# The first rows' second layer begun on three of its four low parts, and three pieces of side work moved in a hybrid decoder step

## The reference, cut to what matters

```
h   = rmsnorm(x);  z = h @ w_in                       # one projection for both head groups
o_g = gated linear attention, 4 heads, 64-token blocks
o_d = (softmax(q1 k1^T) - lambda softmax(q2 k2^T)) v  # 4 heads, causal; the 8 running
                                                      # sequences read 16 cached pages each
x   = x + concat(o_g, o_d) @ w_out
u   = square(relu(rmsnorm(x) @ w_up))                 # 1024 -> 4096
x   = x + u @ w_down                                  # 4096 -> 1024
```

## Time and profile before

| | |
|---|---|
| time, median of 3 runs | 1398.96 us (1396.02 to 1400.2) |
| profiled execution, its own time | 1402.99 us |
| its span, first to last instruction | 1401.3 us |
| PE busy | 1354.2 us (97%) |
| DVE busy | 904.4 us (65%) |
| ACT busy | 576.9 us (41%) |
| POOL busy | 399.6 us (29%) |
| mean granted TensorE clock | 0.994 of full speed |

### The profile page before, as it was taken

How to read it: one execution, slowest core, us unless ns; L and a number is a source line. 1 busy time by engine, 2 the same in 40 slices (tenths; PEclk the granted TensorE clock), 3 DMA queues, 4 the chain that set the end, 5 groups by cost and what they waited for, 6 DMA issues and landing times.

```text
span 1401.3 us, 23890 instructions
## 1 busy us (share of the span) xinstructions
PE 1354.2 (97%) x8589; PEld 1124.1 (80%) x8589; DVE 904.4 (65%) x1624; ACT 576.9 (41%) x1069; POOL 399.6 (29%) x395
## 2 busy tenths in 40 slices
PE   8999999999999989999999999999999999999998
PEld 6867777776777777777767766667999999999998
DVE  5469667745657777647667565525376665878785
ACT  6444333314544654524234241313444454334532
POOL 3546615435533444243000000000252212222020
PEclk9999999999999999999999999999999999999999
DMA  8447745444344665577386675874454564132301
GB/s 287 141 133 235 223 126 169 127 144 131 101 140 157 202 226 149 155 254 257 117 270 219 196 247 175 291 237 155 166 189 160 202 226 164 46 109 106 106 32 61
DMA packets 125543, 239.29 MB, mean 171 GB/s; under 512 B 13601, under 2 KB 46658, under 8 KB 125426
## 3 DMA queue, kind: packets, MB, share of 16 engines
q1 hardware_dynamic: 116226, 213.64, 46.6%
q10 hardware_dynamic: 9200, 24.13, 5.1%
HBM read 197.64 MB, written 40.09 MB: 170 GB/s over the span
## 4 chain that ended last, share of the span: by engine, by line
PE 60%; DVE 7%; issue 3%; ACT 2%; DMA 2%; POOL 1%; SPq 1%; ACTq 0%; DVEq 0%; POOLq 0%
PE ps L87 17%; PE ps L89 16%; PE ps L88 16%; PE ps L3316 2%; PE ps L1513 2%; PE ps L1550 1%; PE ps L1332 1%; DMA kr<-in_cache_k 1%; DVE uw_l L2036 1%; ACT uw_h L2030 1%; DVE sd L3070 1%; PE ps L1534 1%; DVE xt L2854 1%; DMA vr<-in_cache_v 1%; PE ps L1746 1%
## 5 line engine op out<-in xcount | busy, mean ns | idle before, releaser
L3081 POOL TENSOR_TENSOR kr<-kr,qb 128x512 f32<-128x512 f32 x128 | 171.8, 1354 | 171.8 <-DMA kr<-in_cache_k 171.5
L87 PE MATMUL ps<-x2hB,uw_h 128*128 128x264 f32 (+1 forms) x512 | 145.1, 283 | 0.7 <-DVE x2lB L2869 0.7
L88 PE MATMUL ps<-x2lB,uw_h 128*128 128x264 f32 (+1 forms) x512 | 144.7, 283 | 0.0
L89 PE MATMUL ps<-x2hB,uw_l 128*128 128x264 f32 (+1 forms) x512 | 144.5, 282 | 0.0
L87 PE MATMUL ps<-part_h,fh 128*128 128x264 f32 (+1 forms) x448 | 128.1, 286 | 4.5 <-DVE xt L2854 4.5
L89 PE MATMUL ps<-part_h,fl 128*128 128x264 f32 (+1 forms) x448 | 127.0, 284 | 0.0
L88 PE MATMUL ps<-part_l,fh 128*128 128x264 f32 (+1 forms) x448 | 126.9, 283 | 0.0
L87 PE MATMUL ps<-uh,dh 128*128 128x512 f32 x256 | 105.1, 411 | 8.2 <-DVE dl L2129 5.2
L3070 DVE TENSOR_REDUCE sd<-kr 128x8 f32<-128x512 f32 x128 | 85.0, 675 | 38.7 <-POOL kr L3081 38.6
L2854 DVE TENSOR_TENSOR xt<-xt,ps 128x264 f32<-128x264 f32 (+1 forms) x224 | 87.4, 422 | 34.2 <-PE ps L89 33.9
L87 PE MATMUL ps<-x2hA,uw_h 128*128 128x512 f32 x256 | 105.2, 411 | 0.0
(11 more groups left out here) (383 smaller groups left out, 3436.3 us busy)
## 6 DMA issues: line engine op xcount, KB each, us to landing
kr<-in_cache_k SPq DMA_DIRECT2D x128, 256.0 KB, 3.3
raw_up<-in_w_up_units SPq DMA_DIRECT2D x64, 512.0 KB, 4.7
vr<-in_cache_v SPq DMA_DIRECT2D x128, 256.0 KB, 3.6
raw_dn<-in_w_down SPq DMA_DIRECT2D x32, 512.0 KB, 6.3
raw_dn<-in_w_down ACTq DMA_DIRECT2D x32, 512.0 KB, 5.0
raw<-in_w_in_units SPq DMA_DIRECT2D x23, 512.0 KB, 5.7
raw_up<-in_w_out_units SPq DMA_DIRECT2D x16, 512.0 KB, 4.4
kept_up_low<-uw_l SPq DMA_DIRECT2D x14, 512.0 KB, 6.5
```

The source lines that it names most:

```text
L87: pe.matmul(out, lh, rh, start=first and n == 0, stop=False, skip_group_check=onto)
L88: pe.matmul(out, lh, rl, start=False, stop=False, skip_group_check=onto)
L89: ins = pe.matmul(out, ll, rh, start=False, stop=last and n == len(ks) - 1, skip_group_check=onto)
L3081: pool.tensor_tensor(k[:, :], k[:, :], qb[v // PAGES][:, :], ALU.mult).then_inc(k_multiplied, 1)
```

## The change

It does five things. `down` waits for three `dl` at its top and for the fourth, together with the fourth `ul`, after the six partial sums. ScalarE's side work of tick 19 stands ahead of the square of tile 1 of group 0 instead of behind its high part. VectorE's side work of tick 38 (tile 3 of group 1) stands behind `dl`, `xr` and `ul` instead of ahead of them. VectorE's side work of the ticks of group 1's `down` stands behind each addition instead of ahead of it. Step 13 of `keysB` moves from tick 16 to tick 17, where step 14 already stands.

```diff
         def down(g, tick):
-            pe.wait_ge(dn_low, FT * g + FT)
+            pe.wait_ge(dn_low, FT * g + 3)
             pe.wait_ge(u_low, up_no(g, 2) + 1)
...
             for o in range(2):
                 take(pe, "down", g, o)
                 sum_over(o, range(3), True, False)
+            pe.wait_ge(dn_low, FT * g + FT)
+            pe.wait_ge(u_low, up_no(g, 3) + 1)
             for o in range(2):
-                pe.wait_ge(u_low, up_no(g, 3) + 1)
                 sum_over(o, range(3, 4), False, True).then_inc(down_ready, 1)
...                                                    # scalar
+                if g == 0 and x == 1:
+                    beside(tick + 2 * x + 1)
                 i = up_no(g, x)
                 v = vt[:, i % 2, ALL]
                 act.wait_ge(v_made, i + 1)
                 act.activation(v, v, ACT.Square).then_inc(u_high, 1)
...
-                beside(tick + 2 * x + 1)
+                if g or x != 1:
+                    beside(tick + 2 * x + 1)
...                                                    # vector
-                beside(tick + 2 * x)
+                pages_last = (g, x) == (1, FT - 1)
+                if not pages_last:
+                    beside(tick + 2 * x)
                 down_low(g, x)
...
+                if pages_last:
+                    beside(tick + 2 * x)
                 beside(tick + 2 * x + 1)
...
             for o in range(KT):
-                beside(tick + 2 * FT + o)
+                if g != 1:
+                    beside(tick + 2 * FT + o)
                 dve.wait_ge(down_ready, down_no(g, o) + 1)
                 dve.tensor_tensor(xt[:, o, ALL], xt[:, o, ALL], ps[:, bank("down", g, o), :], ALU.add).then_inc(added, 1)
+                if g == 1:
+                    beside(tick + 2 * FT + o)
...                                                    # program: the table of ticks
-        put("keysB", [t0 + 2 + 41 * i // 37 for i in range(37)])
+        put("keysB", [t + (t == t0 + 2 * KT) for t in (t0 + 2 + 41 * i // 37 for i in range(37))])
```

## The result

The changed kernel takes 1403.04 us (median of 13 runs, 1400.47 to 1405.85), the kernel before 1399.09 us in the same runs. The ratio is 1.0028, with a 95% interval of 1.0020 to 1.0035. So it is about 4 us slower: a small loss, but the interval doesn't hold 1. The forecast was 1402.0, 3 us slower.

The account below looks back on a forecast made before the run. TensorE was taken as the bound, with a VectorE chain deciding from 506 to 513.5 us. Group 0 +6.4, group 1 -3.0 and the `down` split -0.4 gave +3.0 us on 1398.96: 1402.0 us, range 1396.5 to 1406.5.

Parts of the forecast that it names:

- The round trip of the key page: Group 0, VectorE at tick 18: waiting for page 92 takes 6.0 us from page 90's sum and delays `dl`.
- the normalisation: Group 0, POOL: the root starts earlier with the key product behind it, gaining 0.6 us (0.45 to 1.32).
- `stat`: Group 0, VectorE: this 1.05 us instruction no longer runs beside a POOL product, saving 0.7 us (0 to 0.8).
- the mix and the turn of unit 7: Group 0, VectorE then TensorE: both come 4.7 us later (bounds 3.4 to 8.5).
- ScalarE's edit: Group 0: `attn_t` is copied earlier, but TensorE then waits as much longer for the mix; cost and gain 0.
- The clock: Group 0, TensorE: the granted clock falls after an 8 us idle stretch, costing 1.7 us (0 to 3).
- the one precedent: Earlier trace: after a 2.88 us TensorE wait before 10.27, the clock was 0.72 from 10 to 16, losing 1.7 us.
- Group 1: TensorE's waits for `dl` and additions shrink, key page 112 then being late: gain 3.0 us (0.4 to 3.4).
- The split of `down`: Groups 2, 3 and 5: starting on three low parts gives 0.4 us in all (0 to 0.73).
- the two additions: Groups 3 and 5: first additions end a VectorE and ScalarE chain from `dl`, so removed waits return; gain 0.
- the 0.4 us counted for group 2: TensorE starts `down` 0.73 us earlier, but the addition of output 0 lets it keep only 0.4 us.
- The sum: Whole kernel: +6.4 - 3.0 - 0.4 = +3.0 us, giving 1402.0 us against the median; chance 50%.

Follow-up runs that it names:

- experiment 1: Kernel before with only key step 13 moved from tick 16 to tick 17: 1404.53 us, ratio 1.0039.
- experiment 2: Changed kernel with key step 13 put back at tick 16: 1399.23 us, ratio 0.9998 against the kernel before.
- experiment 5: Changed kernel with key step 15 also moved, from tick 18 to 19, behind the mix of unit 7: 1403.91 us, ratio 1.0037 against the kernel before.
- experiment 8: Kernel before with only ScalarE's side work of tick 19 moved ahead of the square: 1400.32 us, ratio 1.0008.
- Experiment 6: Changed kernel with 32 unused matmuls filling TensorE's long wait before the turn of unit 7: 1402.73 us, ratio 1.0027 against the kernel before.
- experiment 4: Kernel before with only group 1's VectorE side work moved behind `ul` and behind the additions: 1396.52 us, ratio 0.9982.
- experiment 3: Kernel before with only `down` begun on three of the four low parts: 1399.45 us, ratio 1.0002.
- experiment 7: Changed kernel with `down` begun on all four low parts again: 1404.19 us, ratio 1.0041 against the kernel before.
- experiment 9: Kernel before with only POOL's root of the normalisation moved ahead of its tick 16 side work: 1398.48 us, ratio 0.9991.
- experiment 10: Kernel before with group 1's VectorE side-work edits and POOL's root ahead of tick 16's side work: 1395.56 us, ratio 0.9969.
- experiment 11: Kernel before with group 1's edits, early root, `down` begun on three low parts, and output 0's addition earlier in every group: 1395.81 us, ratio 0.9971.
- experiment 12: Kernel before with group 1's edits, early root, split `down`, earlier output 0 addition, and ScalarE's tick 19 ahead of the square: 1395.91 us, ratio 0.9979.

## Why the prediction was right, point by point

**The round trip of the key page** was the right mechanism, shown by experiments 1, 2 and 5. No run gives the ring a third buffer, which would test it most directly. Its size came out right for a partly wrong reason, by luck. I had taken 6.0 us from the end of the sum of page 90 to the sum of page 92; it took 4.8 us (501.5 to 506.25), as the transfer took 2.57 us and not 3.4. The formula that the prediction quotes from the Trainium skill ("DMA: Bandwidth & Descriptors", Anatomy of one DMA) is given there for transfers that GpSimd issues, while SP issues these. Its 2.6 us fits the transfer of key page 92, and not that of key page 112, which took 5.0 us. What I had left out made up for the shorter trip. `dl` took 2.00 us instead of 1.2 and `ul` 1.81 instead of 0.7, each issued while POOL had just begun a product (506.51 and 510.80). In the prediction's own sum the terms were 6.0 for the trip, -0.6 for the normalisation and -0.7 for `stat`. They measured 4.8, -1.4 and -0.8, with 0.8 more for `dl` and 1.1 for `ul`: the mix and the turn of unit 7 came 4.5 us later, and I had said 4.7.

**The normalisation** gained the whole 1.3 us, not 0.6. I had put the value near the low end because the root took 2.00 us beside VectorE's splitting. In the changed kernel the root began 0.12 us ahead of the split of `uw_l`, took 1.02 us, and the split took 1.23 us (1.21 at 509.38, with POOL idle). By the rule of the Trainium skill ("SBUF — State Buffer", Who interferes with whom) the split should have been held until the root was over. It wasn't, so for this pair the trace disagrees. For `dl` and `ul` it agrees: `dl`, issued at 506.86 into a product that ends at 507.77, lasted until 508.86, 1.1 us after it.

**ScalarE's edit** gave nothing (experiment 8), for the reason stated.

**The clock** fell as the one precedent had let expect, for longer: 2.7 us in the trace instead of 1.7. Experiment 6 shows that the idle stretch is the cause of this fall: filled with work, it had none. In the same trace the clock fell a second time, in group 3 behind the wait of 2.19 us, which the prediction doesn't have:

```profile
718.00:720.00 2.00, 2.00 (x6) 1.57 (x5) 2.00 (x6) 0.88 (x2) 0.00 (x0) 0.52 1.03 405
720.00:722.00 2.00, 2.00 (x10) 1.29 (x9) 1.33 (x4) 1.44 (x2) 0.00 (x0) 0.63 1.05 381
```

**Group 1** was mis-sized in the changed kernel: of 3.4 us of waits 2.0 are left, a gain of 1.4 us instead of 3.0, as the round trip of key page 112 took 7.8 us. Alone the edits gave 2.7 us (experiment 4). What varied was the round trip, which I had seen range from 5.5 to 8.9 us; the forecast took 6.3 for it, and 8.9 only as a bound.

**The split of `down`** gave 0 in groups 3 and 5, as worked out from the two additions and shown by experiment 3. Of the 0.4 us counted for group 2 the traces show 0.05, and in all it gave nothing measurable.

**The sum.** Predicted +3.0 us, measured +4.0. The single edits measured against the kernel before give +5.3 + 0.2 - 2.7 + 1.4 = +4.2 us, each of them uncertain by 1.3 to 2 us. That forecast and time lie so near is in part luck: group 0 cost 7.2 us in the trace (forecast 6.4), group 1 gave back 1.4 (3.0) and the split nothing (0.4), which alone makes +5.8.

The two profiled executions differ by +6.5 us in block A, more than the medians do, and much of the excess is the clock, which doesn't fall alike in every execution. Experiments 3 and 4 don't touch group 0. TensorE has the same wait of 1.9 us for `attn_t` there, yet the clock fell behind it, and `down` of group 0 begins 0.9 us later than in the trace of the kernel before, which kept 1.00. In experiment 3:

```profile
508.00:510.00 2.00, 0.47 (x2) 0.47 (x3) 1.74 (x4) 1.74 (x6) 1.16 (x1) 0.91 1.00 261
510.00:512.00 2.00, 2.00 (x12) 2.00 (x11) 1.96 (x3) 1.06 (x1) 0.51 (x1) 0.50 0.96 354
512.00:514.00 2.00, 2.00 (x12) 1.87 (x12) 1.90 (x3) 0.53 (x2) 0.00 (x0) 0.74 1.04 412
```

The second fall in the changed kernel adds to it: from group 3's `down` to group 4's its trace takes 66.7 us, and experiment 3's, with the same split and no fall there, 66.0. Without these two the difference would be about 4.9 us, an estimate. The rest stays open.

## What to carry to other kernels

When a step of a pipelined side job is moved next to its neighbour, count the round trip of its buffer ring: with two buffers, everything between step `s` and step `s`+2 must last as long as a transfer and its processing, or an in-order engine stops there with all its other work. A wait that ends on an engine with its own chain (here `dl`, `ul`, the addition) wasn't removed by starting its user earlier. It came back under the next name with the same length, so look for what the chain itself depends on. Before a difference of 1 us between two traces is put down to an edit, compare the granted clock over the same stretch: here it fell in one execution and not in another with the same waits. Here the useful part of a coupled edit could be had by moving one instruction on the one engine where the conflict was.

## What the hardware showed that I had not expected

A root of 128x4 on POOL took 1.02 us beside VectorE's 128x1024 subtraction that began 0.12 us after it, and neither slowed the other. Seven more traces (experiments 5 to 7 and 9 to 12) show the same pair at 1.01 to 1.03 and 1.23 us. In the kernel before, the same root took 2.00 us when it began 0.55 us behind that subtraction, which itself began beside a product on POOL:

```profile
496.89 1.67 DVE L2036 TENSOR_TENSOR uw_l<-raw_up,uw_h 128x1024 fp32r<-128x1024 f32 x1 [0.20 <-ACT uw_h L2030]
```

In experiment 1, with no product there, the root began 0.16 us behind the subtraction and took 1.93 us, and the subtraction 1.22.

The granted clock fell behind waits shorter than the 2.88 us of the earlier trace rows, and not each time. Six kernels have TensorE's wait of 1.9 us for `attn_t` in group 0. Before and in experiments 9 and 11 the clock stayed at 1.00 behind it; in experiments 3, 4 and 10 it fell, to 0.50 or 0.51 in one window of 2 us. Behind one wait of 2.7 to 2.8 us at the same place (experiments 2, 5, 8 and 12) it fell in all four.
